# The second mixer's attention on split operands in permuted strips, with its bias table assembled early

## What is computed

```python
def neighbourhood_attention(q, k, v, k_ctx, v_ctx, rpb):     # 8 heads of 64; tokens are a grid of 8 rows x 64 columns
    c0 = np.clip(cols - kc // 2, 0, GRID_W - kc)             # 16 columns around the query's own, all 8 rows
    bias = rpb[:, row_off, col_off]                          # learned, by relative row and column
    s_loc = einsum(q_r, k_nb) + bias
    s_ctx = einsum(q_r, k_ctx)                               # 256 context tokens as well
    p = softmax(concatenate([s_loc, s_ctx]))
    ...
o_a = neighbourhood_attention(to_heads(q_a) * scale, to_heads(k_a), to_heads(v_a), k_ca, v_ca, rpb)
qb = axial_rope(rmsnorm(to_heads(q_b), g_qn), row, col) * scale      # 8 query heads
kb = axial_rope(rmsnorm(to_heads(k_b), g_kn), row, col)              # 2 key heads
o_b = blocked_gqa(qb, concatenate([kb, k_cb]), concatenate([v_b, v_cb]))   # 512 + 256 keys
y = (sigmoid(g_a) * (o_a @ w_out_a) + sigmoid(g_b) * (o_b @ w_out_b)) @ w_o
```

## Time and profile before

| | us |
|---|---|
| runs | 3282.76, 3286.60, 3290.73 (median 3286.6) |
| profiled execution | 3282.52, its span 3280.8 |
| TensorE busy | 2668.0 (81% of the span) |
| VectorE busy | 2247.1 (68%) |
| ScalarE busy | 1519.0 (46%) |
| GpSimd busy | 301.4 (9%) |
| mean granted TensorE clock | 0.878 of 2.4 GHz |

### The profile page before, as it was taken

One profiled execution on the slowest core, in us unless ns is written; L12 is line 12 of the kernel. 1 busy time (PEld: TensorE's weight loads), 2 busy tenths in 40 slices (PEclk: granted clock), 3 DMA queues, 4 the chain that ended last, 5 costly groups with the idle time before them and its releaser, 6 DMA issues. The chain is left out here.

```text
span 3280.8 us, 38147 instructions
## 1 busy us (share of the span) xinstructions
PE 2668.0 (81%) x12972; PEld 2125.4 (65%) x12972; DVE 2247.1 (68%) x2162; ACT 1519.0 (46%) x1375; POOL 301.4 (9%) x263
## 2 busy tenths in 40 slices
PE   2957965489994499479978359999999999999991
PEld 2844635377773399446657347777787877877771
DVE  5566656378785411356542579999999999999985
ACT  2222120167672323124432136777677776777760
POOL 0100000023321000000000000011111011111110
PEclk9985557599997699789999569999999999999995
DMA  5613511289994322020021159999999999999994
GB/s 205 232 30 141 167 26 59 104 323 371 362 383 172 103 65 95 24 46 1 1 103 52 53 208 355 369 366 359 366 371 366 368 354 366 371 367 366 359 352 147
DMA packets 261961, 732.14 MB, mean 223 GB/s; under 512 B 34995, under 2 KB 75122, under 8 KB 261810
## 3 DMA queue, kind: packets, MB, share of 16 engines
q1 hardware_dynamic: 237394, 654.41, 55.3%
q0 software_dynamic: 19872, 72.39, 5.8%
q10 hardware_dynamic: 4608, 4.20, 0.4%
HBM read 693.16 MB, written 37.80 MB: 223 GB/s over the span
## 5 line engine op out<-in xcount | busy, mean ns | idle before, releaser
L48 PE MATMUL psum_all<-sb_ring_r,sb_arena_r 128*128 128x512 f32 (+1 forms) x2912 | 1071.2, 368 | 0.0
L152 DVE TENSOR_TENSOR sb_ring_r<-sb_ring,sb_hi_ring 128x2048 fp32r<-128x2048 f32 x297 | 674.2, 2286 | 278.8 <-ACT sb_hi_ring L143 273.2
L47 PE MATMUL psum_all<-sb_hi_ring,sb_arena_r 128*128 128x512 f32 (+1 forms) x1880 | 664.8, 354 | 58.0 <-DVE sb_ring_r L152 55.1
L49 PE MATMUL psum_all<-sb_hi_ring,sb_arena_r 128*128 128x512 f32 (+1 forms) x1880 | 659.5, 351 | 0.0
L143 ACT ACTIVATE sb_hi_ring<-sb_ring 128x2048 fp32r<-128x2048 f32 x297 | 564.2, 1914 | 119.4 <-DMA sb_ring<-in_w_gu_dram 36.4
L48 PEld LDWEIGHTS psum_all<-sb_ring_r,sb_arena_r 128*128 128x128 f32 x2912 | 557.4, 191 | 91.6
L152 DVE TENSOR_TENSOR sb_ring_r<-sb_ring,sb_arena_r 128x2048 fp32r<-128x2048 f32 x258 | 581.8, 2283 | 31.0 <-ACT sb_arena_r L143 30.8
L143 ACT ACTIVATE sb_arena_r<-sb_ring 128x2048 fp32r<-128x2048 f32 x258 | 486.2, 1915 | 198.3 <-DMA sb_ring<-in_w_gu_dram 194.0
L47 PEld LDWEIGHTS psum_all<-sb_hi_ring,sb_arena_r 128*128 128x128 f32 x1880 | 359.5, 191 | 114.8 <-DVE sb_ring_r L152 55.7
L47 PE MATMUL psum_all<-sb_arena_r 128*128 128x512 f32 x1032 | 415.2, 402 | 11.9 <-DVE sb_ring_r L152 6.9
L49 PE MATMUL psum_all<-sb_arena_r 128*128 128x512 f32 x1032 | 412.0, 399 | 0.0
(11 more groups left out here) (311 smaller groups left out, 2879.6 us busy)
## 6 DMA issues: line engine op xcount, KB each, us to landing
sb_ring<-in_w_gu_dram SPq DMA_DIRECT2D x272, 1024.0 KB, 6.8
sb_ring<-in_w_dn_dram SPq DMA_DIRECT2D x136, 1024.0 KB, 9.5
sb_ring<-in_w_e_gate_dram SPq DMA_DIRECT2D x36, 1024.0 KB, 7.4
sb_ring<-in_w_e_up_dram SPq DMA_DIRECT2D x36, 1024.0 KB
sb_ring<-in_w_e_down_dram SPq DMA_DIRECT2D x36, 1024.0 KB, 8.1
sb_ring<-in_w_in_dram SPq DMA_DIRECT2D x27, 1024.0 KB, 5.8
sb_ring<-in_w_mod_dram SPq DMA_DIRECT2D x24, 1024.0 KB, 5.8
sb_arena<-in_w_ada_dram POOLq DMA_DIRECT2D x16, 1024.0 KB, 5.6
```

The source lines that it names most:

```text
L47: eng.matmul(out, a[0], b[0], start=start, stop=False)
L48: eng.matmul(out, a[0], b[1], start=False, stop=False)
L49: return eng.matmul(out, a[1], b[0], start=False, stop=stop)
L152: dve.tensor_tensor(s.lo[c % SLOTS], s.raw[c % SLOTS], s.hi[c % len(s.hi)].bitcast(F32), ALU.subtract).then_inc(s.lo_made, 1)
```

## The change

The tokens of the second mixer are kept in another order: strips of 16 grid columns, 8 rows each, so that one tile of 128 is one strip. `turn` takes an `order` for that on the way in ("t2") and out ("tz"), and the rotary tables are permuted on the host. With strips, a query tile needs the keys of its own and of the adjacent strips alone: 2 strips + context (512 keys) for the first and last tile, 3 strips + context (640 keys) for the two in the middle.

`attention` for "na" and "gq" becomes `attend` (block one keeps `attention`), with one unit per tile and head, tile by tile. Operands are halves in fp32r: queries and keys, probabilities and values. Probabilities are not scaled; four heads' results are divided at once (`put`). Results leave as halves, so `split_tiles` goes. `attend` makes the transposes of the grouped branch itself, so "tq", "tk" and "tkc" go. To have both halves of the query in one contraction of 128, `rotate_heads` writes each head twice (ScalarE copies it, `again`). Step u of each engine:

`neighbour_bias` goes. Its table is made early:

```diff
 setup
+            sp.dma_start(pad[:, 0:RPB_PAD], zeros).then_inc(s.padded, 16)
+            sp.dma_start(pad[:, RPB_PAD + size:], zeros).then_inc(s.padded, 16)
+            sp.dma_start(pad[:, RPB_PAD:RPB_PAD + size], a["rpb_2"].rearrange("o h r c -> o (h r c)")).then_inc(s.padded, 16)
+            sp.wait_ge(s.padded, 48)
 modulation
+        @block.scalar
+        def _(act):
+            for p in range(P):
+                first = RPB_PAD + (WIN_R - 1 - p // 16) * RPB_C + (WIN_C - 1 - p % 16) - 16
+                src = bass.AP(k.rpb_pad.tensor, first, [[RPB_R * RPB_C, NH], [RPB_C, GRID_H], [1, 48]])
+                act.dma_start(k.rpb_rows[p], src).then_inc(k.rpb_rows_stored, 16)
 gates_and_lru, GpSimd
+            pool.wait_ge(s.rows_loaded, 32)
+            for w, first in enumerate((16, 0, 16, 32, 16)):
+                for h in range(NH):
+                    pool.tensor_tensor(table[:, w, h], rows[:, GRID_H * h:GRID_H * (h + 1), first:first + 16],
+                                       wide(window[:, w], 1, GRID_H), ALU.add).then_inc(s.masked, 1)
 gates_and_lru, SyncE
+            sp.wait_ge(k.rpb_rows_stored, 16 * P)
+            sp.dma_start(k.ring[:, 0:2, :]..., k.rpb_rows...).then_inc(s.rows_loaded, 16)
+            sp.dma_start(k.ring[:, 5, 0:80], a["window_mask"]...).then_inc(s.rows_loaded, 16)
+            sp.wait_ge(s.masked, 5 * NH)
+            sp.dma_start(k.rpb_table, ...).then_inc(s.table_stored, 16)
+            sp.wait_ge(s.table_stored, 16)
 rotate_heads
+            for t in range(ntt):
+                act.wait_ge(s.rotated, (t + 1) * len(outs))
+                act.activation(again[1](t), again[0](t), ACT.Copy)
-                    dve.tensor_tensor(o[:, :, :, 0], p1, p2, ALU.subtract)
+                    link(dve.tensor_tensor(o[:, :, :, 0], p1, p2, ALU.subtract))
                     link(dve.tensor_tensor(o[:, :, :, 1], p3, p4, ALU.add))
 block_two_mixer
-                 [(4 * g, 4, lambda t, g=g: q_kv[:, t, g]) for g in range(2)], scratch, tables)
+                 [(0, NH, lambda t: qr[:, t, :, 0, :])], scratch, tables,
+                 (lambda t: qr[:, t, :, 0, :], lambda t: qr[:, t, :, 1, :]))
```

More of the change, by code:

```diff
@@ L200, in setup @@
     with stage(nc) as ctx:
-        s = sems(nc, ctx, "set", "loaded", "x_loaded", "made", "turned", "copied", "sig", "done", "silu")
+        s = sems(nc, ctx, "set", "loaded", "x_loaded", "made", "turned", "copied", "sig", "done", "silu", "zero", "padded")
         row_tile = k.arena[0:nrows, 0:P]
@@ L483, in _, with turn @@
             act.activation(rstd, inv, ACT.Sqrt).then_inc(s.root, 1)
-def turn(nc, k, name, src, ntt, nk, scale, shift, hi, lo, plain=None, ahead=()):
+def turn(nc, k, name, src, ntt, nk, scale, shift, hi, lo, plain=None, ahead=(), order=None):
     n = ntt * P
@@ L686, in gates_and_lru @@
                  "decay", "chain", "tanh_a", "inner", "tanh", "variance", "root", "cubic",
-                 "f_loaded", "split", "multiplied", "biased", "exp")
+                 "f_loaded", "split", "multiplied", "biased", "exp", "rows_loaded", "masked", "table_stored")
+        rows = k.ring[:, 0:2, :].rearrange("p a n -> p (a n)")[:, 0:NH * GRID_H * 48].rearrange("p (m c) -> p m c", c=48)
+        table = k.ring[:, 2:5, :].rearrange("p a n -> p (a n)")[:, 0:NH * 5 * P].rearrange(
+            "p (h w r c) -> p w h r c", h=NH, w=5, r=GRID_H)
+        window = k.ring[:, 5, 0:80].rearrange("p (w c) -> p w c", w=5)
         w_f = k.rows[:, 0, 512:512 + KD * NH].rearrange("p (k h) -> p k h", k=KD)
@@ L1855 @@
 RPB_SIZE = NH * RPB_R * RPB_C + 2 * RPB_PAD
-NDR = 14
 KV = 128
@@ new lines, in _, with to_grid, from_grid, probabilities @@
+                    dve.sem_inc(s.rotated, 1)
+def to_grid(out, psum):
+    return (out.rearrange("p (g r c) -> p r g c", g=TT, r=GRID_H), psum.rearrange("p (r g c) -> p r g c", r=GRID_H, g=TT))
+def from_grid(out, psum):
+    return (out.rearrange("p (r g c) -> p g r c", r=GRID_H, g=TT), psum.rearrange("p (g r c) -> p g r c", g=TT, r=GRID_H))
+def probabilities(k):
+    probs = k.rows
+    hi = k.hi_ring[:, 2, 0:2 * 768].rearrange("p (b n) -> p b n", b=2)
+    lo = k.arena_r[:, 2048:2048 + 2 * 768].rearrange("p (b n) -> p b n", b=2)
+    tmp = k.arena[:, 24064:24320].rearrange("p (h d) -> p h d", h=4)
+    return probs, (hi, lo), k.pair, tmp
@@ L2020, in block_two_mixer @@
     normalise(nc, k, "n2", k.x, TT, D, xn, False, 1e-6)
-    turn(nc, k, "t2", xn, TT, KD, k.mod["sc1_2"], k.mod["sh1_2"], *u)
+    turn(nc, k, "t2", xn, TT, KD, k.mod["sc1_2"], k.mod["sh1_2"], *u, order=to_grid)
     ctx_x, ctx_n = area(0, TC, D), area(2048, TC, D)
@@ L2094, in block_two_mixer @@
-    turned = k.arena[:, 2048:2048 + 2 * KEYS].rearrange("p (b g n) -> p b g n", b=2, n=P)
-    units = []
-    for h in range(NH):
-        rows, j = slice(HD * (h % 2), HD * (h % 2) + HD), h // 2
-        for t in range(TT):
-            q = qa[rows, j, t * P:(t + 1) * P]
-            first = NDR - GRID_H - 2 * t
-            units.append(dict(
-                products=[(slice(0, T), q, ka[rows, j, 0:T], True, True),
-                          (slice(T, KEYS), q, ka[rows, j, T:KEYS], True, True)],
-                bias=table[:, h, first:first + GRID_H, :].rearrange("p j c -> p (j c)"), n=KEYS,
-                v=[va[:, g, h * HD:(h + 1) * HD] for g in range(TT + TC)], out=oa[rows, j, t * P:(t + 1) * P]))
@@ L2106, in block_two_mixer @@
-    attention(nc, k, "na", units, probs, turned)
-    units = []
-    for h in range(NH):
-        kv = h // 4
-        rows = slice(HD * kv, HD * kv + HD)
-        for t in range(TT):
-            q = qbt[rows, h % 4, t * P:(t + 1) * P]
-            units.append(dict(
-                products=[(slice(0, T), q, kbt[rows, 0, 0:T], True, True),
-                          (slice(T, KEYS), q, kbt[rows, 0, T:KEYS], True, True)],
-                bias=None, n=KEYS, v=[kvb[:, g, KV + HD * kv:KV + HD * kv + HD] for g in range(TT + TC)],
-                out=ob[HD * (h % 2):HD * (h % 2) + HD, h // 2, t * P:(t + 1) * P]))
@@ L2120, in block_two_mixer @@
-    attention(nc, k, "gq", units, probs, turned)
-    oat = (area(16384, 4, T, F32R), area(18432, 4, T, F32R))
-    obt = (area(20480, 4, T, F32R), area(22528, 4, T, F32R))
-    split_tiles(nc, k, "so", [(oa, *oat), (ob, *obt)],
-                ahead=[column_chunk(a["w_out_a_2"][0], 512 * h, 512) for h in range(AHEAD)])
+                 [(0, 2, lambda t: kr[:, t, :, 0, :])], scratch, tables,
+                 (lambda t: kr[:, t, :, 0, :], lambda t: kr[:, t, :, 1, :]))
+    oat = (area(15360, 4, T, F32R), area(17408, 4, T, F32R))
@@ L2145, in block_two_mixer @@
     y = area(12288, TT, D)
-    turn(nc, k, "tz", z, TT, KD, None, None, *zt,
+    turn(nc, k, "tz", z, TT, KD, None, None, *zt, order=from_grid,
          ahead=[column_chunk(a["w_o_2"][0], 256 * h) for h in range(AHEAD)])
```

446 lines of the change are left out of this document (361 added, 85 removed).

## The result

The changed kernel takes 3302.3 us (median of 20 runs), the kernel before 3288.6 in the 20 runs beside it: ratio 1.0036, with a 95% interval of 1.0021 to 1.0052. It is slower by 0.4%. The profiled execution has a span of 3308.5 us against 3280.8, 27.7 more, at a mean granted clock of 0.870 against 0.878.

A forecast was written before the change was run, and what follows sets the result against it. TensorE set attention's steady step, 3.74 us; bias stage and turns were largely waiting. Terms -52.6 - 1.5 - 11.4 - 3.9 + 27 + 4 + 1 = -37, from 3286.6 to 3250 us; range 3210 to 3306.

The forecast's parts named there:

- price of a row DMA: First modulation stage: ScalarE issues 128 DRAM-to-DRAM DMAs at 0.46 us each, 59 us, +27 us beyond the cover.
- rival A: First modulation: row DMA issue at 0.99 us each, +95 instead of +27, 3318 us; decides from about 0.75; chance 0.16.
- Stages gone: Bias stage (34.8 us), turns (9.1) and split stage (8.7) leave with their barriers: -52.6 us.
- rotate_heads: The two rotations: 4 wider query groups instead of 8, extra ScalarE copies mostly hidden; -1.5 us, ends -3 and +2.
- na: Neighbour attention: steps of 3.1 and 2.8 us, lead 11.6, tail 9; 112 us against 123.4, -11.4.
- Rival B: Both attention stages: TensorE falls to the lower clock, +69 us, less perhaps 20; 3300 us; chance 0.13.
- gq: Grouped attention: 9.3 us lead, 31 steps of 3.2, 9.5 behind; 118 us against 121.9, -3.9.
- Loop: Attention steps: exponent, transposes, rounding and handovers take 2.46 us (640 keys), 2.2 (512), 2.7 (grouped); VectorE level in neighbour attention.
- Recurrent stage: Table assembly by 40 GpSimd additions hidden there, slowing VectorE's critical path: +4 us, between 0 and 18.
- Rival D: Recurrent stage: additions and VectorE hold each other up and the table's store ends late; +25 us, 3275; chance 0.06.
- Setup, permuted access: Three more DMAs in setup, +1 us (0 to +3); permuted ScalarE reads in two turns, 0 (up to +4).

The follow-up runs named there:

- e3: The changed kernel with each row DMA copying 8 runs of 265 elements instead of 64 runs of 48; 3291.9 us, ratio 1.0012 to the kernel before.
- e4: The changed kernel with each row DMA copying one contiguous run of 3520 elements; 3290.9 us, ratio 1.0005 to the kernel before.
- h1: The changed kernel with each row DMA copying one run into an SBUF partition, then one store to DRAM; 3303.8 us, ratio 1.0036 to the kernel before.
- e1: The changed kernel with one DMA of the same size instead of 128, leaving out the table's contents; 3231.6 us, ratio 0.9829 to the kernel before.
- f2: The changed kernel with ScalarE taking exponent u before rounding the probabilities of u-1, in both stages; 3377.4 us, ratio 1.0276 to the kernel before.

## Why the prediction was wrong

I forecast 3250, faster; it is 3302, inside the range, on the other side. The failed step is the **price of a row DMA**: I took 0.46 us (+27); it is 0.718 from one to the next (+61), and this is 34 of the 45 us between -37 and the +8 below. That is rival A, in milder form than its 0.99. Its point of decision, 0.75, was too high: 0.718 lies under it, and the kernel is slower all the same. It counted on 64 us gained elsewhere, and 53 came (61 less 8), which puts it at 0.66; by the medians, 13.7 us apart, it is 0.61 (both estimates). What failed in the reasoning is the scale I put the rows on: number of runs. e3 and e4 show that runs hardly matter from DRAM to DRAM. I had set the row that was nearest in kind, DRAM to DRAM at 0.96, at the end of the range because it was a single one, and had let ScalarE's cheap row, whose transfer goes from SBUF to DRAM, pull the estimate down. h1, with its 0.27 at first, shows that the kind of a DMA can more than double the price at the same source and size. The rule on engines in the Trainium skill (DMA: Bandwidth & Descriptors) would have pulled it down too, toward the low end, and the measurement went the other way.

The steps one by one:

- *Stages gone*: right, to a tenth.
- *rotate_heads*: -1.5 was expected, 0.1 came; my range went to +2. A tile of the queries comes every 2.49 us, near the 2.4 I had for a wider group; I take it that the copies and the second rotation's waits ate the rest, which no run shows.
- *"na"*: the step was right: with the clock up (e1) the 31 steps take 91.9 us, against 16 x 3.1 + 15 x 2.8 = 91.6; the lead is 11.0 (11.6), the tail 9.7 (9). What the sum left out is the fall of the clock after the hole at a finished tile. Rival B had the effect, for the whole of both stages; it came in pieces of up to 20 us, at the holes of one stage. The term I had at nothing is this hole, 2.2 us twice, and what the clock does behind it. "gq" has at most falls of about 3 us in its steps, and at their start and end both stages are partly at 0.50 in every profile. Over the seven profiles "na" is 118.2 us on average, 6 over the 112.
- *"gq"*: steps (3.2) and tail (9.6) right, the lead 11.2 instead of 9.3. A steady step is 2.69 us, as the loop gave it:

```profile
1645.77 0.91 ACT L1128 ACTIVATE sb_rows<-psum_all,sb_small 128x768 f32<-128x768 f32 x1
...
1647.71 0.87 ACT L1119 ACTIVATE sb_hi_ring<-psum_all 128x512 fp32r<-128x512 f32 x2 [0.94 <-PE psum_all L1061]
1648.46 0.91 ACT L1128 ACTIVATE sb_rows<-psum_all,sb_small 128x768 f32<-128x768 f32 x1
```

- *Loop*: that it sets the step together with VectorE was right in size. In "gq" the rows above show it; in "na" with the clock up (e1) the exponent waited for VectorE's maximum 16 times, 9.7 us in all. But what I drew from it for f2 was wrong: it left out that VectorE, too, works in order, so that a remainder waiting for ScalarE holds up the next maximum.
- *Recurrent stage*: +4 was forecast, 2.1 came. The Trainium skill (SBUF — State Buffer, Who interferes with whom) has the two engines contend; they do, 680 to 825 ns. But VectorE lost that only on its small instructions: beside the large ones it was GpSimd's addition that took longer, up to 5.90 us, and the upper end of 18 was far off. Rival D fell.
- *Setup, permuted access*: 0.1 and nothing to be seen, as taken.

With +61.1 in the DMA term, 118.2 for "na" (-5.2), and "gq" (-0.9), rotation, recurrent stage, setup and other stages as profiled, the sum against the median of 3286.6 is +8, 3294; the measured ratio gives 3298.4. The rest of the 27.7 us between the two profiled executions is block one's attention and a "na" with both falls: chance of those two executions.

## What to carry to other kernels

A DMA's issue is a price on the engine that issues it, 0.27 to 0.63 us here by the kind of DMA, and from DRAM to DRAM nearly the same for 8.3 and for 13.8 KB. So a stage with many small DMAs can be as long as their number times that price: measure it on the very kind of DMA, count them, spread them over the queues, and put them where the barrier does not wait. In a software pipeline over several engines, ask of each instruction that waits what is queued behind it. A pause of TensorE costs twice when the clock falls after it, as it did in some profiles and not in others; put work that others depend on ahead of the instruction that waits.
